# A two-layer streaming encoder step on one core: the end of the recurrence in an order of its own on each engine, and the norms between stages with ScalarE squaring from the bank, outputs weighted as they leave it, and rows taken in twos

## The chip, the core and the metric

The kernel runs on one NeuronCore of a Trainium2 chip. Five engines work at the same time, each through its own list of instructions in order: TensorE (PE, matrix products, with its weight loads PEld beside it), VectorE (DVE), ScalarE (ACT), GpSimd (POOL) and SyncE (SP, which here only issues DMAs). They meet through semaphores. The metric is the device time of one execution in microseconds; the kernel before takes 2728.57 us, the median of 3 runs.

## The reference

288 tokens (256 of a prompt, 32 of a running stream) go through two layers, D_MODEL = 2048, all in float32. Layer 0 mixes by a gated linear recurrence with 16 heads of 128, layer 1 by latent attention. Each mixer and each ConvFFN stands between two RMS norms:

```python
def rms_norm(x, w):
    y = xf * lax.rsqrt(jnp.mean(xf * xf, axis=-1, keepdims=True) + EPS)
    return (y * w.astype(F32)).astype(x.dtype)
...
    h = rms_norm(x, norm_w[layer, 0])
    m, s = hgrn2_mixer(h, ...)            # or mla_mixer in layer 1
    x = x + rms_norm(m, norm_w[layer, 1])
    f, buf = conv_ffn(rms_norm(x, norm_w[layer, 2]), ...)
    x = x + rms_norm(f, norm_w[layer, 3])
```

In the recurrence each head gives `o`, which is normalised by itself (`rms_norm(o, g_norm_w) * silu(g)`) and enters the product with `w_out` as one of its 16 rows of 128.

## The kernel before, in words

Features lie on the 128 partitions and tokens along the free axis, so an activation is 16 rows of 128x288 (`X`, `Y`). Every float32 product is made of three: a weight chunk `raw` (up to 8 blocks of 128x128, 512 KB) is split by ScalarE into `w_hi` (`split_hi`, L216) and by VectorE into the rest `w_lo` (`split_lo`, L223), and `product` runs hi*hi, hi*lo and lo*hi (L229 to L231). Chunks go round a ring of four; a chunk's `w_hi` waits until TensorE has done the chunk four before (`chunk_done`). A tile of output (128 features) is two chunks in most products; four banks of PSUM hold tiles 0 to 3 in turn.

**The recurrence** is a loop over heads. In step j TensorE makes the four input tiles of head j (`mm(0)` to `mm(7)`), while VectorE, ScalarE and GpSimd work on head r = j-1 (gates, decays, operands; `main`) and t = j-2 (scores, states, output; `tail`). Between its chunks TensorE turns values (L617), makes state updates (L625), the head's output (L634 to L639), the sum of squares of it (L646, L650), turned keys (L656) and the score products (L668 to L672). The last two steps, j = 16 and 17, are the same code with fewer parts: in j = 16 the chunks are those of the next product, `hgrn_out` (`late(0)` to `late(7)`, by `gemm_late`, rows 0 to 13 of its 16), and in j = 17 nothing is left but head 15's tail, with `late(8)` before the head's output and `late(9)`, the product of its last row, at the very end. VectorE applies the scores (`att`, L493 to L509) before TensorE may go on to the updates. SU, GS and OV, which hold updates, sum and output, lie in the same banks as the scores; TR has a bank of its own.

**Output tiles** of `hgrn_out`, `mla_out` and the four `ffn_out` phases leave the bank by ScalarE into `yt` (`out_act`, L725). VectorE copies them to `Y` (L741) or adds them (L737, second half of an FFN), squares them (L739, L742) and sums the squares (`ssq`, L744). `run_out` sets the order: the splits for tile t, then the drain of tile t-1; after the last trip three splits for the next phase, the last drain, and the fourth split.

**A norm between stages** (s = 1 to 4) begins when TensorE has summed `ssq` over partitions (L871). ScalarE loads the table set (L811), makes the reciprocal root (L806, L808), and then VectorE walks through the 16 rows: `Y` times weight and root (L880), `X` plus `Y` (L884) and, three rows behind, `h_lo` (L889). ScalarE makes `h_hi` and the square of each row (L827, L828). TensorE follows row by row (`gemm_first`): tiles 0 and 1 over rows 0 to 7, then the rest, and after chunk 6 a product with `ssx` (L290), the sum of the squares that VectorE folds at L903. Norm 1 stands behind `hgrn_out`, 2 behind the first FFN, 3 behind `mla_out`; norm 4 ends the program, and its rows go out by one DMA each (L1486).

## Time and profile before

| | |
|---|---|
| median of 3 runs | 2728.57 us (2728.56 to 2728.85) |
| the profiled execution | 2727.83 us, its span 2726.0 us |
| PE busy | 2653.6 us, 97% of the span |
| DVE, ACT, POOL busy | 1809.6, 1279.9, 410.2 us |
| HBM traffic | 406.97 MB read, 151 GB/s over the span |
| TensorE clock granted | 0.990 of full speed in the mean |

The span is from the first to the last instruction; 1.83 us lie around it. A row of the profile names the line, the engine, what is written and read, and, in brackets, how long the engine sat idle just before it and who released it. Idle time of an engine that nobody waits for costs nothing, so TensorE's idle stretches are the ones to follow here.

### The profile page before, as it was taken

The page shows a single profiled execution, that of the slowest core. Times are in us where ns is not written, and L with a number is a line of the kernel's source. Part 1 is how long each engine was busy: PE and PEld are TensorE (multiplying, and loading weights), DVE is VectorE, ACT ScalarE, POOL GpSimd, SP SyncE. Part 2 cuts the span into 40 slices and gives each one's busy share as a digit, 9 for nine tenths or more (in the row PEclk, how much of TensorE's full clock was granted, in tenths as well). Part 3 has the DMA queues.
Part 4 walks back from the last instruction along what each step waited for, and adds up shares of the span by engine and source line. Part 5 has one row for each costly group of instructions (what it writes and reads, how often), then busy time and mean ns, then how long its engine had stood idle before and what let it go on. Part 6 is the DMA issues. An engine that isn't in the chain of part 4 may idle for free.

```text
span 2726.0 us, 55560 instructions
## 1 busy us (share of the span) xinstructions
PE 2653.6 (97%) x19734; PEld 2637.2 (97%) x19734; DVE 1809.6 (66%) x3089; ACT 1279.9 (47%) x2133; POOL 410.2 (15%) x792
## 2 busy tenths in 40 slices
PE   8999999988999999999999999998999999999997
PEld 8999999988999999999999999998999999999997
DVE  7788888757766644766755855558766545666655
ACT  6555666435444433444434566535444433444432
POOL 1111112100322100222200000001322101222200
PEclk9999999999999999999999999999999999999998
DMA  6444444444555555454455422253544555445553
GB/s 230 138 140 137 143 137 130 129 136 137 165 167 165 160 165 169 160 169 162 153 175 168 147 89 81 94 169 128 179 160 165 162 166 166 165 160 168 163 164 112
DMA packets 124256, 413.58 MB, mean 152 GB/s; under 512 B 14032, under 2 KB 22384, under 8 KB 124176
## 3 DMA queue, kind: packets, MB, share of 16 engines
q1 hardware_dynamic: 116064, 406.37, 46.6%
q10 hardware_dynamic: 7056, 3.21, 0.4%
q0 software_dynamic: 1056, 2.92, 0.3%
q8 instruction: 50, 0.82, 0.1%
q14 instruction: 30, 0.25, 0.0%
HBM read 406.97 MB, written 5.48 MB: 151 GB/s over the span
## 4 chain that ended last, share of the span: by engine, by line
PE 92%; DVE 5%; ACT 1%; issue 1%; DMA 0%; POOL 0%; DVEq 0%; ACTq 0%; SPq 0%
PE bank L229 29%; PE bank L231 29%; PE bank L230 29%; DVE Y L880 1%; DVE X L884 1%; DVE w_lo L223 1%; DVE h_lo L889 1%; PE bank L669 1%; PE bank L1430 1%; PE bank L625 1%; DVE Y L903 1%; PE bank L670 0%; PE bank L634 0%; ACT w_hi L216 0%; PE bank L1435 0%
## 5 line engine op out<-in xcount | busy, mean ns | idle before, releaser
L229 PE MATMUL bank<-h_hi,w_hi 128*128 128x288 f32 (+1 forms) x4208 | 1267.4, 301 | 31.2 <-DVE h_lo L889 15.4
L230 PE MATMUL bank<-h_lo,w_hi 128*128 128x288 f32 (+1 forms) x4208 | 1251.0, 297 | 0.0
L231 PE MATMUL bank<-h_hi,w_lo 128*128 128x288 f32 (+1 forms) x4208 | 1247.2, 296 | 0.0
L216 ACT ACTIVATE w_hi<-raw 128x1024 fp32r<-128x1024 f32 (+2 forms) x786 | 807.7, 1037 | 887.1 <-PE bank L231 877.3
L223 DVE TENSOR_TENSOR w_lo<-raw,w_hi 128x1024 fp32r<-128x1024 f32 (+2 forms) x786 | 954.9, 1225 | 376.3 <-ACT w_hi L216 375.5
L229 PEld LDWEIGHTS bank<-h_hi,w_hi 128*128 128x128 f32 x4208 | 791.6, 188 | 37.8 <-issue 29.5
L231 PEld LDWEIGHTS bank<-h_hi,w_lo 128*128 128x128 f32 x4208 | 794.5, 189 | 0.2
L230 PEld LDWEIGHTS bank<-h_lo,w_hi 128*128 128x128 f32 x4208 | 792.8, 188 | 0.7
L1054 POOL TENSOR_TENSOR ext<-yt,small 128x256 f32<-128x256 f32 x176 | 213.3, 1212 | 1533.3 <-ACT yt L949 1035.8
L229 PE MATMUL bank<-g_hi,w_hi 128*128 128x288 f32 x1408 | 416.8, 296 | 0.0
L230 PE MATMUL bank<-g_lo,w_hi 128*128 128x288 f32 x1408 | 415.4, 295 | 0.0
L231 PE MATMUL bank<-g_hi,w_lo 128*128 128x288 f32 x1408 | 413.9, 294 | 0.0
L231 PEld LDWEIGHTS bank<-g_hi,w_lo 128*128 128x128 f32 x1408 | 265.1, 188 | 0.0
L230 PEld LDWEIGHTS bank<-g_lo,w_hi 128*128 128x128 f32 x1408 | 264.2, 188 | 0.0
L229 PEld LDWEIGHTS bank<-g_hi,w_hi 128*128 128x128 f32 x1408 | 263.7, 187 | 0.0
L1009 DVE TENSOR_SCALAR cv<-ext,conv_w 128x290 f32<-128x290 f32 x176 | 77.4, 440 | 216.4 <-POOL conv_new L1060 216.4
L229 PE MATMUL bank<-o_hi,w_hi 128*128 128x288 f32 x512 | 155.5, 304 | 10.8 <-DVE w_lo L223 7.7
L230 PE MATMUL bank<-o_lo,w_hi 128*128 128x288 f32 x512 | 153.7, 300 | 0.0
L231 PE MATMUL bank<-o_hi,w_lo 128*128 128x288 f32 x512 | 153.2, 299 | 0.0
L725 ACT ACTIVATE yt<-bank 128x288 f32<-128x288 f32 x105 | 43.0, 410 | 223.5 <-PE bank L231 223.5
L229 PEld LDWEIGHTS bank<-o_hi,w_hi 128*128 128x128 f32 x512 | 98.7, 193 | 12.0 <-DVE w_lo L223 8.3
L1011 DVE SCALAR_TENSOR_TENSOR cv<-ext,conv_w,cv 128x290 f32<-128x290 f32 x176 | 92.2, 524 | 24.4 <-DVE cv L1009 22.3
(247 smaller groups left out, 2141.6 us busy)
## 6 DMA issues: line engine op xcount, KB each, us to landing
raw<-in_w_fi SPq DMA_DIRECT2D x352, 512.0 KB, 4.0
raw<-in_w_hi_in SPq DMA_DIRECT2D x128, 512.0 KB, 4.2
raw<-in_w_fo SPq DMA_DIRECT2D x128, 512.0 KB, 3.5
raw<-in_w_fo SPq DMA_DIRECT2D x64, 384.0 KB, 3.2
raw<-in_w_ho SPq DMA_DIRECT2D x32, 512.0 KB, 4.1
raw<-in_w_mo SPq DMA_DIRECT2D x32, 512.0 KB, 3.9
raw<-in_w_down SPq DMA_DIRECT2D x18, 512.0 KB, 4.3
raw<-in_w_ukv SPq DMA_DIRECT2D x16, 512.0 KB, 3.8
```

Source lines behind the costliest of these rows:

```text
L216: act.activation(w_hi[:, ch.slot, 0:n], raw[:, ch.slot, 0:n], ACT.Copy).then_inc(hi_done, 1)
L223: dve.tensor_tensor(w_lo[:, ch.slot, 0:n], raw[:, ch.slot, 0:n], w_hi[:, ch.slot, 0:n].bitcast(F32), ALU.subtract).then_inc(lo_done, 1)
L229: pe.matmul(out, w_hi[:, ch.slot, w], rhs_hi, start=start, stop=False)
L230: pe.matmul(out, w_hi[:, ch.slot, w], rhs_lo, start=False, stop=False)
L231: return pe.matmul(out, w_lo[:, ch.slot, w], rhs_hi, start=False, stop=stop)
L625: su = pe.matmul(SU[:, n * P:(n + 1) * P], ktok[0:BL, n, :], vtok[0:BL, min(n, NB - 1), :], start=True, stop=True)
L669: pe.matmul(out[:, A0:A0 + 192], key_a[:, c:c + BL], z[:, OQ:BK], start=True, stop=True)
L725: act.activation(yt[:, t % 4, :], psum[t % 4][:, 0:T], ACT.Copy).then_inc(evacuated, 1)
L880: dve.scalar_tensor_tensor(out=Y[:, k, :], in0=Y[:, k, :], scalar=norm_w[:, la, wa, k:k + 1], in1=RSA, op0=ALU.mult, op1=ALU.mult).then_in ...
L1009: dve.tensor_scalar(cv[:, t, :], ext[:, t, 2:EXT], tap(2), tap(3), ALU.mult, ALU.add).then_inc(conv_step, 1)
L1011: dve.scalar_tensor_tensor(out=cv[:, t, :], in0=ext[:, t, 1:EXT - 1], scalar=tap(1), in1=cv[:, t, :], op0=ALU.mult, op1=ALU.add).then_inc( ...
L1054: pool.tensor_tensor(ext[:, t, 2:2 + TP], yt[:, t, 0:TP], RSB[:, 0:TP], ALU.mult)
```

## The change

It has three parts.

1. **The recurrence's end.** Steps 16 and 17 are replaced by one list per engine: `hgrn_end_act`, `hgrn_end_dve`, `hgrn_end_pe`. The parts of the step became functions of their own (`gate_exps` is L427 to L429 of before, `sigmoids` L431 to L433, `decay_exps` L457 to L459, `diff_exps` L465 to L469, `out_root` L472 to L474; `scores_near` and `scores_far` are L493 to L501 and L509, `differences` L550 to L564, `near_operands` and `far_operands` L576 to L581 and L591 to L593; `turn_values`, `updates`, `head_outputs`, `turn_keys`, `score_products` are the parts of `hgrn_pe`) and hold the same instructions. Head 15's updates go to TR's bank instead of SU's, and the sum of squares of head 14 is one float32 product instead of two split ones.
2. **Drains and norms.** Behind `hgrn_out` and `mla_out` ScalarE squares from the bank into `sq` and then copies from the bank to `Y` times the norm's weight; behind the second half of an FFN VectorE adds the bank to `Y`, ScalarE squares `Y` and weights it in place; the first half goes by ScalarE straight to `Y`. VectorE only sums the squares, and not the last one: TensorE adds `ones` x `ssq` and `ones` x `sq` in the bank. The table set is loaded once, behind the FFNs, ahead of the last drain. In the walk, `Y` and `X` are taken by twos (norms 1 to 3, after two single rows) or by fours and twos (norm 4).
3. **The result** goes out in five DMAs instead of 16.

The diff, cut to its core:

```diff
-            step(eng, HEADS, False, True, True)
-            step(eng, HEADS + 1, False, False, True)
+            end(eng)
+        def hgrn_end_act(act):
+            r, t = HEADS - 1, HEADS - 2
+            hi = lambda k: split_hi(act, "hgrn_out", 0, k)
+            hi(0); hi(1)
+            values_out(act, r)
+            hi(2); hi(3)
+            gates_out(act, r)
+            keys_by_token(act, t)
+            gate_exps(act, r)
+            sigmoids(act, r)
+            hi(4)
+            decay_logs(act, r)
+            hi(5)
+            decay_exps(act, r)
+            states_out(act, t)
+            diff_exps(act, r)
+            out_squares(act, t)
+            state_load(act, r)
+            values_by_token(act, r)
+            hi(6)
+            out_root(act, t)
+            keys_by_token(act, r)
+            out_top(act, t)
+            hi(7)
+            out_squares(act, r)
+            states_out(act, r)
+            out_root(act, r)
+            out_top(act, r)
+        def hgrn_end_dve(dve):
+            lo(0); lo(1); lo(2); lo(3)
+            clamp(dve, r)
+            scores_near(dve, t)
+            gates_keys_queries(dve, r)
+            scores_far(dve, t)
+            decay_sums(dve, r)
+            lo(4)
+            new_states(dve, t)
+            differences(dve, r)
+            lo(5)
+            decayed_keys(dve, r)
+            near_operands(dve, r)
+            far_operands(dve, r)
+            dve.wait_ge(S["o_raw"], t + 1)
+            decayed_queries(dve, r)
+            out_scaled(dve, t)
+            silu_gate(dve, r)
+            lo(6)
+            new_states(dve, r, TR)
+            out_rest(dve, t)
+            lo(7)
+            scores_near(dve, r)
+            scores_far(dve, r)
+            out_scaled(dve, r)
+            out_rest(dve, r)
+        def hgrn_end_pe(pe):
+            late(0)
+            turn_values(pe, r)
+            late(1)
+            late(2)
+            pe.wait_ge(S["att_ready"], t + 1)
+            updates(pe, t)
+            late(3)
+            head_outputs(pe, t)
+            late(4)
+            square_sums(pe, t)
+            turn_keys(pe, r)
+            late(5)
+            pe.wait_ge(S["k_tok"], r + 1)
+            updates(pe, r, TR)
+            score_products(pe, r)
+            late(6)
+            late(7)
+            pe.wait_ge(S["att_ready"], r + 1)
+            head_outputs(pe, r)
+            square_sums(pe, r)
+            late(8)
+            late(9)
...
         def out_act(act, phase, i, t):
+            ycol = Y[:, bass.ds(out_col(phase, i, t), 1), :]
+            bank = psum[t % 4][:, 0:T].unsqueeze(1)
+            if phase not in NORMED:
+                act.wait_ge(chunk_done, last_chunk(phase, i, t))
+                act.activation(ycol, bank, ACT.Copy).then_inc(evacuated, 1)
+                return
+            at = norm_index(phase)
+            if not (isinstance(i, int) and i == 0 and t == 0):
+                act.wait_ge(sums_done, i * TILES[phase] + ((KT - 1) * at + t))
+            if phase in FROM_BANK:
+                act.wait_ge(chunk_done, last_chunk(phase, i, t))
+                act.activation(sq[:].unsqueeze(1), bank, ACT.Square).then_inc(y_squared, 1)
+            else:
+                act.wait_ge(evacuated, tile_number(phase, i, t) + 1)
+                act.activation(sq[:].unsqueeze(1), ycol, ACT.Square).then_inc(y_squared, 1)
+            if not (isinstance(i, int) and out_col(phase, i, t) == KT - 1):
+                weighted(act, phase, i, t)
+        def out_dve(dve, phase, i, t):
+            if phase not in FROM_BANK:
+                dve.wait_ge(chunk_done, last_chunk(phase, i, t))
+                dve.tensor_tensor(ycol, ycol, psum[t % 4][:, 0:T].unsqueeze(1), ALU.add).then_inc(evacuated, 1)
+            if isinstance(i, int) and out_col(phase, i, t) == KT - 1:
+                return
+            dve.wait_ge(y_squared, i * TILES[phase] + (KT * at + t + 1))
+            dve.tensor_tensor(ssq[:], ssq[:], sq[:], ALU.add).then_inc(sums_done, 1)
...
-            load_set(act, EXP_LN_SET)
             if post:
                 rstd(act, stat[s, "post"], psum[4], RSA, D)
+                weighted(act, phase, TRIPS[phase] - 1, TILES[phase] - 1)
...
-            pe.matmul(psum[4][:, 0:T], ones[:], ssq[:], start=True, stop=True).then_inc(n_sum, 1)
+            pe.wait_ge(sums_done, (KT - 1) * s)
+            pe.matmul(psum[4][:, 0:T], ones[:], ssq[:], start=True, stop=False)
+            pe.wait_ge(y_squared, KT * s)
+            pe.matmul(psum[4][:, 0:T], ones[:], sq[:], start=False, stop=True).then_inc(n_sum, 1)
...
+            for g, (k0, n) in enumerate(groups):
+                rows = slice(k0, k0 + n)
+                dve.tensor_tensor(Y[:, rows, :], Y[:, rows, :], RSA.unsqueeze(1).to_broadcast([P, n, T]), ALU.mult)\
+                    .then_inc(y_scaled, n)
+                dve.wait_ge(y_scaled, KT * (s - 1) + k0 + n)
+                dve.tensor_tensor(X[:, rows, :], X[:, rows, :], Y[:, rows, :], ALU.add).then_inc(x_ready, n)
+                if pre and g > 0:
+                    lower(g - 1)
```

`lower(g)` is the `h_lo` step (L889 of before) for the rows of group g, with the two early splits in it as before.

On ScalarE, at the recurrence's end (Y stands for the gates here, ktok for head 14's keys by token), before:

```order
L420 ACTIVATE ktok<-bank 96x256
L421 ACTIVATE ktok<-bank 64x128
L422 ACTIVATE ktok<-bank 32x128
L216 ACTIVATE w_hi<-raw 128x1024
L427 ACTIVATE Y<-Y 128x288
L428 ACTIVATE Y<-row_tiles 128x288
L429 ACTIVATE Y<-row_tiles 128x288
L431 ACTIVATE Y<-Y 128x864
L433 ACTIVATE Y<-Y 128x864
L216 ACTIVATE w_hi<-raw 128x1024
```

and now:

```order
L414 ACTIVATE ktok<-bank 96x256
L415 ACTIVATE ktok<-bank 64x128
L416 ACTIVATE ktok<-bank 32x128
L420 ACTIVATE Y<-Y 128x288
L421 ACTIVATE Y<-row_tiles 128x288
L422 ACTIVATE Y<-row_tiles 128x288
L426 ACTIVATE Y<-Y 128x864
L428 ACTIVATE Y<-Y 128x864
L216 ACTIVATE w_hi<-raw 128x1024
L432 ACTIVATE row_tiles<-row_tiles 128x288
```

The split of the fifth chunk stood ahead of the three exponentials of the gates and the two passes of the sigmoids, and now stands behind them.

On TensorE, where the scores of head 15 are made, before:

```order
L669 MATMUL bank<-Y,row_tiles 96x192
L670 MATMUL bank<-Y 96x144
L672 MATMUL bank<-Y 96x32
L625 MATMUL bank<-vtok,ktok 128x128 x4
L229 MATMUL bank<-o_hi,w_hi 128x288
L230 MATMUL bank<-o_lo,w_hi 128x288
L231 MATMUL bank<-o_hi,w_lo 128x288
```

and now:

```order
L231 MATMUL bank<-o_hi,w_lo 128x288
L752 MATMUL bank<-vtok,ktok 128x128 x4
L792 MATMUL bank<-row_tiles 96x48
L793 MATMUL bank<-Y,row_tiles 96x192
L794 MATMUL bank<-Y 96x144
L796 MATMUL bank<-Y 96x96
L792 MATMUL bank<-row_tiles 96x48
```

Head 15's updates (ktok with vtok) stood behind its scores and now stand ahead of them; behind the scores stood the updates, and stand now the products of two chunks.

On VectorE, at the start of the walk through the rows in norm 1 (small is the reciprocal root), before:

```order
L880 SCALAR_TENSOR_TENSOR Y<-Y,norm_w,small 128x288 x2
L884 TENSOR_TENSOR X<-X,Y 128x288
L880 SCALAR_TENSOR_TENSOR Y<-Y,norm_w,small 128x288
L884 TENSOR_TENSOR X<-X,Y 128x288
L880 SCALAR_TENSOR_TENSOR Y<-Y,norm_w,small 128x288
L884 TENSOR_TENSOR X<-X,Y 128x288
L889 SCALAR_TENSOR_TENSOR h_lo<-X,norm_w,h_hi 128x288
L880 SCALAR_TENSOR_TENSOR Y<-Y,norm_w,small 128x288
```

and now:

```order
L1094 TENSOR_TENSOR Y<-Y,small 128x288
L1097 TENSOR_TENSOR X<-X,Y 128x288
L1094 TENSOR_TENSOR Y<-Y,small 128x288
L1097 TENSOR_TENSOR X<-X,Y 128x288
L1081 SCALAR_TENSOR_TENSOR h_lo<-X,norm_w,h_hi 128x288
L1094 TENSOR_TENSOR Y<-Y,small 128x576
L1097 TENSOR_TENSOR X<-X,Y 128x576
L1081 SCALAR_TENSOR_TENSOR h_lo<-X,norm_w,h_hi 128x288
L1094 TENSOR_TENSOR Y<-Y,small 128x576
```

The first `h_lo` came after seven instructions and now comes after four; the weight is no longer an operand of the first pass, and the passes over `Y` and `X` cover 576 elements from the third row on.

## Rows read from the trace of the kernel before

**Rows 1.** The page, part 1: busy time of TensorE
```profile
PE 2653.6 (97%) x19734; PEld 2637.2 (97%) x19734; DVE 1809.6 (66%) x3089; ACT 1279.9 (47%) x2133; POOL 410.2 (15%) x792
```

**Rows 2.** Waits of TensorE over the whole span: total us, times, longest
```profile
PE bank L229 <- DVE h_lo L889: 15.4, 11, 4.7
...
PE bank L229 <- DVE w_lo L223: 10.5, 6, 4.4
PE bank L871 <- DVE ssq L744: 7.4, 4, 2.0
```

**Rows 3.** Stretches: length, busy PE, PEld, DVE, ACT, POOL, clock, DMA share, GB/s
```profile
509.60:559.30 49.70, 37.82 (x267) 36.57 (x266) 32.55 (x87) 20.53 (x41) 0.92 (x1) 0.91 0.26 84
638.30:671.50 33.20, 25.92 (x171) 24.45 (x170) 31.64 (x62) 23.41 (x45) 0.00 (x0) 0.90 0.32 107
...
700.00:1400.00 700.00, 700.00 (x5252) 700.00 (x5251) 442.95 (x625) 291.10 (x409) 150.44 (x329) 1.00 0.52 165
```

**Rows 4.** Timeline of TensorE, recurrence's end: start us, duration us, what, [idle before]
```profile
519.47 1.05 PE L625 MATMUL bank<-vtok,ktok 96*128 96x128 f32 x8
...
543.20 2.03 PE L625 MATMUL bank<-vtok,ktok 96*128 96x128 f32 x8 [4.72 <-DVE lev L509]
...
553.09 0.40 PE L229 MATMUL bank<-o_hi,w_hi 128*128 128x288 f32 x1 [3.07 <-DVE o_lo L597]
...
559.32 0.61 PE L229 MATMUL bank<-o_hi,w_hi 128*128 128x288 f32 x1 [3.28 <-DVE w_lo L223]
```

**Rows 5.** Timeline of GpSimd and of ScalarE in the same stretch
```profile
509.07 1.45 POOL L681 TENSOR_TENSOR row_tiles<-row_tiles,small 128x288 f32<-128x288 f32 x1 [0.30 <-ACT row_tiles L417]
...
513.00 1.06 ACT L216 ACTIVATE w_hi<-raw 128x1024 fp32r<-128x1024 f32 x1 [3.32 <-PE bank L231]
...
549.18 0.45 ACTq L447 DMA_DIRECT2D o_hs<-s_new  x1
```

**Rows 6.** Timeline of VectorE in the same stretch
```profile
540.68 2.37 DVE L509 COPY_PREDICATED lev<-level_mask,bank 96x144 f32<-96x144 uint32 x6 [0.47 <-issue]
...
558.05 2.35 DVE L223 TENSOR_TENSOR w_lo<-raw,w_hi 128x1024 fp32r<-128x1024 f32 x2
```

**Rows 7.** Timeline around norm 1: ScalarE, VectorE, TensorE
```profile
638.67 1.05 ACT L216 ACTIVATE w_hi<-raw 128x1024 fp32r<-128x1024 f32 x1
...
642.04 0.95 DVE L880 SCALAR_TENSOR_TENSOR Y<-Y,norm_w,small 128x288 f32<-128x288 f32 x2 [0.91 <-ACT small L808]
...
644.87 0.51 DVE L889 SCALAR_TENSOR_TENSOR h_lo<-X,norm_w,h_hi 128x288 fp32r<-128x288 f32 x1
645.30 0.51 DVE L880 SCALAR_TENSOR_TENSOR Y<-Y,norm_w,small 128x288 f32<-128x288 f32 x1
645.73 0.45 DVE L884 TENSOR_TENSOR X<-X,Y 128x288 f32<-128x288 f32 x1
646.10 0.51 DVE L889 SCALAR_TENSOR_TENSOR h_lo<-X,norm_w,h_hi 128x288 fp32r<-128x288 f32 x1
...
666.23 4.74 DVE L903 TENSOR_TENSOR Y<-Y 128x2304 f32<-128x2304 f32 x3
...
671.52 0.51 PE L290 MATMUL bank<-ssx,ones 128*128 128x288 f32 x1 [0.35 <-DVE ssx L903]
```

**Rows 8.** Durations of VectorE additions by size in norm 1
```profile
L903 DVE TENSOR_TENSOR Y<-Y x3: 757/1359/2551, 666.2 to 670.2; 128x2304 f32<-128x2304 f32 x1, 128x1152 f32<-128x1152 f32 x1, 128x576 f32<-128x576 f32 x1
```

**Rows 9.** Timeline: ScalarE before norm 2, TensorE in mla_out
```profile
1495.70 0.41 ACT L725 ACTIVATE yt<-bank 128x288 f32<-128x288 f32 x1 [1.28 <-PE bank L231]
...
1497.07 1.28 ACT L811 ACT_TABLE_LOAD   x1
...
1770.48 0.61 PE L229 MATMUL bank<-o_hi,w_hi 128*128 128x288 f32 x1 [4.42 <-DVE w_lo L223]
```

**Rows 10.** Timeline of norm 4 on VectorE, and its DMAs
```profile
2710.88 0.95 DVE L880 SCALAR_TENSOR_TENSOR Y<-Y,norm_w,small 128x288 f32<-128x288 f32 x2 [1.85 <-ACT small L808]
...
o_y<-X SPq DMA_DIRECT2D x16, 144.0 KB, 1.7
```

More of the change, by code:

```diff
@@ new lines, in turn_values, with updates @@
+        def turn_values(pe, r):
+            pe.wait_ge(S["scaled"], 4 * r + 3)
+            if past_first(r):
+                pe.wait_ge(S["k_tok"], r)
+            for n in range(NB):
+                tr = pe.transpose(TR[0:BL, n * P:(n + 1) * P], vfm[:, n * BL:(n + 1) * BL], ident[:])
+            tr.then_inc(S["v_turned"], 1)
+        def updates(pe, t, su=SU):
+            for n in range(NB + 1):
+                up = pe.matmul(su[:, n * P:(n + 1) * P], ktok[0:BL, n, :], vtok[0:BL, min(n, NB - 1), :], start=True, stop=True)
+            up.then_inc(S["updates"], 1)
@@ L709, in trunk_program @@
-        for name, trips, _, tiles in order:
-            if "out" in name or "down" in name:
-                mode = {"hgrn_out": "only", "mla_out": "only", "down": "first"}.get(name)
-                mode = mode or ("first" if name.endswith("0") else "add")
-                y_count[name] = (n_done, n_kept, n_sq, mode)
-                n_done += trips * tiles
-                n_kept += trips * tiles if mode == "add" else 0
-                n_sq += trips * tiles if mode != "first" else 0
         TRIPS = {name: trips for name, trips, _, _ in order}
+        NORMED = {"hgrn_out": (0, 1), "ffn_out01": (0, 3), "mla_out": (1, 1), "ffn_out11": (1, 3)}
@@ L719, in out_act, with norm_index @@
+        FROM_BANK = ("hgrn_out", "mla_out")
+        def norm_index(phase):
+            return list(NORMED).index(phase)
         def out_act(act, phase, i, t):
[L720 to L725 removed]
@@ L748, in run_out @@
+        def run_out(eng, phase, split, drain, ahead=lambda: None):
             trips, n = TRIPS[phase], TILES[phase]
@@ L762, in run_out @@
             split_next(eng, split, phase, (0, 1, 2))
+            ahead()
             drain(eng, phase, trips - 1, n - 1)
@@ L932, in ffn_act @@
             stats = half == 0 and isinstance(i, int) and i == 0
-            before = {(0, 0): "hgrn_out", (0, 1): "ffn_out00", (1, 0): "mla_out", (1, 1): "ffn_out10"}[layer, half]
-            y_before = y_count[before][0] + TRIPS[before] * TILES[before]
             def hi(t):
```

607 lines of the change are left out of this document (323 added, 284 removed).

## The prediction

> **What bounds the kernel now.** I read the page first: TensorE is busy for 2653.6 us of the 2726.0 us span [rows 1], so all there is to gain lies in the 72 us in which it is idle and in the time at the lower clock. The table of its waits comes next: 15.4 us for `h_lo`, 10.5 us for `w_lo`, 7.4 us for `ssq` [rows 2]. The table by stretch tells where: in an FFN the engine never stops (5252 products in 700 us, so they start 0.133 us apart, at 2.4 GHz), while the recurrence's end has 37.8 us of work in 49.7 us, at a granted clock of 0.91 [rows 3]. The timelines of single stretches give the rest. I work from five places: the recurrence's end, norms 1 to 3 with the drains ahead of them, the start of `mla_out`, norm 4, and everything else as cover.
>
> **1. The recurrence's end.** Before, TensorE starts `late(0)` at 509.6 and the first product of the next trip at 559.32. Its idle pieces in between are 4.72 us (scores of head 15), about 0.8 us in two small waits, 3.07 us (last row) and 3.28 us (first `w_lo` of the next trip) [rows 4], 11.9 us in sum, as rows 3 have it (49.70 less 37.82). Three pieces run at 1.2 GHz: the updates at 543.20 take 2.03 us where those of head 14 took 1.05 us [rows 4], and two times 12 products 0.11 us longer each; some 3.5 us less the few that were fast already, so 3.0. That leaves 49.7 - 11.9 - 3.0 = 34.8 us of work.
> The new order, by the durations of before: the exponentials of the gates waited until 514.0 behind a split that had itself waited 3.32 us for TensorE, until 513.00 [rows 5]; their own input is there at 509.07 + 1.45 = 510.5 [rows 5]. So gates, sigmoids, decays and differences all come 3 to 5 us earlier; on TensorE the scores need no wait and come 3.6 us earlier, at 531.9, for the updates (0.9 us) now stand ahead of them and the two chunks of `late(6)` and `late(7)` (2 x 18 products, 4.8 us) behind. VectorE needs 4.5 us from the scores' end to the last mask (from 543.20 - 4.72 = 538.5 to 540.68 + 2.37 = 543.05 [rows 4, 6]), and these 4.8 us hide it: the wait of 4.72 us goes, and the slow clock behind it. What is late next is the chain behind head 15's output. From 549.2, where its sum of squares starts and ScalarE issues the second DMA, to the last row at 553.09 are 3.9 us [rows 4, 5]: sum, root, two VectorE steps, `o_hi` and `o_lo`. TensorE's own 0.6 us in it and `late(8)`, 1.6 us, which now follows the sum, hide 2.2; the root waits 0.2 for the two DMA issues, as the sum now runs fast: 1.9 us idle is left. Then the drains of the first trip. ScalarE squares tile 0, VectorE sums it, and only then may the next square start: 0.41 + 0.46 and two hand-overs, 0.95 us per tile, but VectorE has one addition per tile and not three instructions. I take the square and the weighting at the 0.41 us of the copy from the bank [rows 9]; 0.5 each would add 0.3. First `w_lo`: 0.6 + 2 x 0.95 + 0.85 (square and weighting of the third tile) + 1.05 + 1.2 = 5.5 us behind the start of `late(9)`, against 559.32 - 553.09 = 6.2 us; idle 3.9 us, and slow behind it as before. New time: 34.8 + 0.35 (float32 sum instead of split) + 0.5 (square) + 0.15 (turned keys wait for `vtok`) + 1.9 + 3.9 = 41.6 us, against 49.7: **-8.1 us**. In the chain three hand-overs have a slack of only 0.1 to 0.5 us (keys by token, last mask, `w_lo` of the eighth chunk). Ends: each late by a microsecond, -5; all of the wait at `late(9)` hidden, -10.
>
> **2. Drains and norms 1 to 3.** Behind `hgrn_out` the chain was: ScalarE copy, three VectorE steps, L871, table load, root, first row at 642.04 [rows 7]. Squares now come from ScalarE alone, the sum over 15 tiles is in the bank before the last one comes, and the load is gone. But the fourth split of the next phase stands between: `w_hi` at 638.7 for 1.05 us [rows 7], `w_lo` behind it for 1.2 (2.35 for two [rows 6]), until 641.0, and VectorE starts its rows there: -1.0 us (norm 3 alike). In norm 2 VectorE's addition stays ahead of the square, so the split starts 0.5 us later: -0.7.
> The walk. From first row to L290 it took 671.52 - 642.04 = 29.5 us [rows 7]: per row 0.43 (L880) + 0.37 (L884) + 0.43 (L889) = 1.23 [rows 7], 16 of them, four splits 4.5 us, the fold 5.2 us. Now a pair has `Y`, on which `X` waits at once: 0.757 us for 576 elements [rows 8] and 0.03, then 0.67, then two `h_lo`, 0.86: 2.31 us, 1.16 per row. 7 pairs, two single rows of 1.29 each, splits and fold: 28.6 us, **-0.9 each**. The first `h_lo` is ready at 2.2 us instead of 3.3 us, row 7 at 11.1 instead of 11.9. TensorE has 120 products (16.0 us) between row 7 and L290 and could be there at 28.0, so VectorE's fold still decides, and a slow clock in rows 0 to 7 is hidden up to 0.6 us. Sum: norms 1 and 3 -1.9 each, norm 2 -1.6: **-5.4 us**. Ends: nothing from the walk, -2.7; the fold no longer last, -7.
> On size the Trainium skill (VectorE: DVE Perf Modes, "The TRN2 errata") says that a fixed latency is paid per instruction and is worth amortising over 512 elements and more; its fixed term of 151 cycles fits the rows within 2 ns (757 and 1359 ns [rows 8]). Paid in full for each of the 14 instructions saved per norm, that would be an estimate of 2.2 us a norm. The rows show 0.43 and 0.37 from start to start where the durations are 0.51 and 0.45 [rows 7], so most of it was overlapped before, and I stay with 0.9.
> The table load of 1.28 us [rows 9] behind the FFNs now stands before the last drain, where ScalarE sat idle for 1.28 us before its copy [rows 9] and now waits 0.5 us longer for VectorE: hidden. The Trainium skill (ScalarE: Activation LUTs, "What ACT_TABLE_LOAD costs") counts 2.66 us for a switch, with a drain; by that, 0.9 us would show in norm 2 and my sum would be 0.9 less.
>
> **3. Start of `mla_out`.** TensorE waits 4.42 us for `w_lo` [rows 9], from 1766.06, behind three drains on VectorE. By the count of part 1 (first bank full 1.1 us before that, 2 x 0.95 + 0.85 + 1.05 + 1.2 = 5.0) it comes at 1769.9 instead of 1770.48: **-0.6**. Ends 0 and -1.
>
> **4. Norm 4.** No split stands in it: TensorE's wait of 2.0 us for `ssq` [rows 2] becomes an addition (0.46) and a square (0.41): the first row comes 1.0 us earlier than 2710.88 [rows 10]. No rows after it feed TensorE. 16 rows took 16 x 0.80 = 12.8 us (0.43 + 0.37 [rows 7]). Fours take 1.36 + 0.02 + 1.27 = 2.65, twos 1.45: 3 x 2.65 + 2 x 1.45 = 10.9 us, -1.9. The last DMA is twice as large; at the 1.7 us to landing for 144 KB [rows 10] I add 0.5. **-2.4**. Ends -1.2 and -3.
>
> **Everything else.** ScalarE gets two instructions per tile (0.9 us) and loses one, VectorE loses two or three. Both are far from full in the FFN (443 and 291 us of 700 [rows 3]), and a chunk's `w_lo` is ready some 3 us after the drain, while TensorE has 6.4 us of work or more ahead: nothing, but about 0.3 us per tile if that cover were gone.
>
> **Sum**: 8.1 + 5.4 + 0.6 + 2.4 = 16.5 us. 2727.83 - 16.5 = 2711.3 for an execution like the profiled one; the median of the runs is 0.7 us above it, so **2712 us**, 0.6% faster.
>
> **Rivals.**
> A. *The clock.* With rows in twos TensorE gets 12 products in 2.3 us, with gaps, and may stay at 1.2 GHz until row 7: 48 products cost 0.24 each, row 7 ends at 14.6 instead of 12 and L290 comes at 30.6 instead of 28.6. Against it: over norm 1 the clock was 0.90 [rows 3], so 6.6 of 33.2 us stood at the low level, most of them before the first row; it rose while the rows came singly, with gaps. Three norms lose 2.0 each: 2718. The Trainium skill (TensorE: Matmul & The Clock Gate, Part 1) calls the low rate the default that activity releases; it speaks for this rival, and no row shows rows in twos.
> B. *A new wait in the recurrence's end.* ScalarE's list is strict: `decay_exps` waits for head 14's states, so the differences' exponentials may come late, the scores with them, and the 4.8 us of cover are spent. Half of part 1 goes: 2716.
> C. *More than that.* After shorter idle stretches the clock stays up where trips start (2.1 us each at `hgrn_out` and `mla_out`), and half of the last-row wait is hidden: 2707.
> D. *Slower.* TensorE stays at 1.2 GHz through norms 1 to 3 beyond row 7. That costs rival A's 2.0 us and 120 x 0.107 = 12.8 us a norm, in full 44 us: 2756. It decides from 33 slow products behind row 7 in each norm, where 16.5 us are spent. 48 products without a gap follow row 7, which speaks against it.
> E. *The walk gains nothing*, since the wait of `X` on `Y` shows in full on each pair: -2.7 us less gain, 2715.
>
> **Chances.** Forecast 0.50 (2709 to 2714 its own range), A 0.14, B 0.12, C 0.10, E 0.11, D 0.03. From 2706 to 2719 leaves out D and the tails of the others, together below 0.2, and takes in the ends of each part taken singly. A difference under about 0.2% (5.5 us) can't be told from none here: faster by more needs below 2723. All single cases but D stand there; A, B and E together would reach it, 0.03: faster 0.94, same 0.03, slower 0.03.
>
> **What would show it.** Right: no wait of TensorE for the masks (4.72 us before) and the first product of the next trip near 551; the exponentials of the gates at 510.6; L290 28.6 us behind the first row of each norm; the first row of norm 1 right behind the fourth `w_lo`; 10.9 us for norm 4's rows. Wrong: a new TensorE wait above 1 us between 527 and 540; L290 with TensorE never waiting for it (rival A); VectorE pairs longer than 2.4 us; a table load between the last drain and a root.

## The result, and the profile after

The changed kernel takes 2712.19 us (median of 5 runs, 2711.43 to 2713.47) against 2728.57 us (5 runs, 2728.05 to 2730.66): a ratio of 0.9937, 95% interval 0.9926 to 0.9948, 16.4 us less. The forecast was 2712. The profiled execution has a span of 2711.6 us, 14.4 less than before. Below, "after" is this kernel.

The page's first part and TensorE's waits over the span, as in [rows 1, 2]:

```profile
PE 2656.3 (98%) x19742; PEld 2639.2 (97%) x19742; DVE 1759.4 (65%) x2892; ACT 1300.3 (48%) x2173; POOL 410.7 (15%) x792
```
```profile
PE bank L229 <- DVE h_lo L1081: 12.1, 8, 3.7
...
PE bank L229 <- DVE w_lo L223: 10.5, 6, 3.8
...
PE bank L1068 <- ACT sq L905: 1.2, 2, 0.6
PE bank L290 <- DVE ssx L1111: 0.9, 3, 0.3
```

`h_lo` went from 15.4 to 12.1 us, the wait of 7.4 us for `ssq` became 1.2 us for `sq`, and the masks (4.72 us, [rows 4]) have no row any more. `w_lo` is where it was in sum.

To place the gain I cut both traces at the same instructions: start of `late(0)`, first product behind the wait at the next trip, last product of `hgrn_out` (or of the FFN, or of `mla_out`), first row of the norm on VectorE, and L290.

| from, to (us) | before | after | difference | forecast |
|---|---|---|---|---|
| start, `late(0)` | 509.47 | 510.88 | +1.41 | 0 |
| `late(0)`, next trip's first product | 49.85 | 40.92 | -8.93 | -8.1 |
| to the last product of `hgrn_out` | 78.71 | 78.29 | -0.42 | 0 |
| last product, first row: norms 1 and 3, each | 4.01 | 2.93 | -1.08 | -1.0 |
| the same, norm 2 | 4.06 | 3.44 | -0.62 | -0.7 |
| first row, L290: norms 1 to 3, each | 29.48 | 29.15 | -0.33 | -0.9 |
| L290 of norm 2, first product of the next trip in `mla_out` | 241.54 | 240.90 | -0.64 | -0.6 |
| to the last product of `mla_out` | 78.97 | 79.07 | +0.10 | 0 |
| last product, first row of norm 4 | 4.08 | 3.24 | -0.84 | -1.0 |
| first row of norm 4, end | 15.12 | 13.81 | -1.31 | -1.4 |

The two FFNs take 823.86 us each, as before (823.85). The rows sum to -14.4 us, which is the span's. The first is no work of the change. Both kernels begin with the same list of products, 0.24 us apart at 1.2 GHz; before, the clock rises at 14.06 us (the duration falls from 0.44 to 0.35), after it does so at 17.06, some 12 products later, each 0.107 us longer, and the first had started 0.12 us later. TensorE's timeline of before, then of after:

```profile
13.82 0.44 PE L230 MATMUL bank<-h_lo,w_hi 128*128 128x288 f32 x1
14.06 0.35 PE L231 MATMUL bank<-h_hi,w_lo 128*128 128x288 f32 x1
```
```profile
16.82 0.43 PE L230 MATMUL bank<-h_lo,w_hi 128*128 128x288 f32 x1
17.06 0.33 PE L231 MATMUL bank<-h_hi,w_lo 128*128 128x288 f32 x1
```

In the eleven kernels below the clock rose between 14.2 and 17.1 us, with the same instructions up to there. Without that row the change gave 15.8 us in the traces.

The stretches that answer to [rows 3] (length, busy PE, PEld, DVE, ACT, POOL, clock, DMA share, GB/s): the recurrence's end, the rest of `hgrn_out`, norm 1.

```profile
510.88:551.80 40.92, 35.09 (x269) 34.23 (x267) 30.50 (x80) 20.34 (x42) 1.03 (x1) 1.00 0.31 102
551.80:630.09 78.29, 78.29 (x576) 78.29 (x577) 35.96 (x38) 32.94 (x48) 0.00 (x0) 0.98 0.51 168
630.09:662.17 32.08, 27.55 (x175) 25.50 (x174) 29.40 (x45) 21.50 (x38) 0.00 (x0) 0.89 0.36 115
```

TensorE is idle for 5.8 us of the recurrence's end, where it was 11.9, and the clock is 1.00 where it was 0.91. Its three waits there, on TensorE's timeline (answering to [rows 4]), and the exponentials of the gates on ScalarE's ([rows 5]):

```profile
542.27 0.75 PE L769 MATMUL bank<-yt,ones 128*128 128x288 f32 x2 [0.50 <-ACT yt L436]
...
546.10 0.40 PE L229 MATMUL bank<-o_hi,w_hi 128*128 128x288 f32 x1 [1.49 <-DVE o_lo L671]
...
551.80 0.40 PE L229 MATMUL bank<-o_hi,w_hi 128*128 128x288 f32 x1 [3.84 <-DVE w_lo L223]
```
```profile
511.95 0.44 ACT L420 ACTIVATE Y<-Y 128x288 f32<-128x288 f32 x1 [0.86 <-POOL row_tiles L860]
```

ScalarE's drains of the first trip (L902 square, L915 weighted copy), which replace L725, and what stands behind them:

```profile
546.80 0.41 ACT L902 ACTIVATE sq<-bank 128x288 f32<-128x288 f32 x1 [1.25 <-PE bank L231]
547.11 0.50 ACT L915 ACTIVATE Y<-bank,norm_w 128x288 f32<-128x288 f32 x1
547.81 0.41 ACT L902 ACTIVATE sq<-bank 128x288 f32<-128x288 f32 x1 [0.20 <-DVE ssq L930]
...
548.74 0.41 ACT L902 ACTIVATE sq<-bank 128x288 f32<-128x288 f32 x1
...
549.43 2.00 ACT L216 ACTIVATE w_hi<-raw 128x1024 fp32r<-128x1024 f32 x2
```

Squares follow each other after 1.01 and 0.94 us; `w_hi` waits behind three of them, and TensorE for its `w_lo`.

Norm 1 on VectorE (answering to [rows 7]): two single rows, a pair in the middle, the fold; then L290 on TensorE.

```profile
633.02 0.45 DVE L1094 TENSOR_TENSOR Y<-Y,small 128x288 f32<-128x288 f32 x1
...
633.50 0.46 DVE L1097 TENSOR_TENSOR X<-X,Y 128x288 f32<-128x288 f32 x1
...
637.13 0.75 DVE L1094 TENSOR_TENSOR Y<-Y,small 128x576 f32<-128x576 f32 x1
637.99 0.76 DVE L1097 TENSOR_TENSOR X<-X,Y 128x576 f32<-128x576 f32 x1
638.66 0.94 DVE L1081 SCALAR_TENSOR_TENSOR h_lo<-X,norm_w,h_hi 128x288 fp32r<-128x288 f32 x2
639.52 0.75 DVE L1094 TENSOR_TENSOR Y<-Y,small 128x576 f32<-128x576 f32 x1
...
656.88 4.74 DVE L1111 TENSOR_TENSOR Y<-Y 128x2304 f32<-128x2304 f32 x3
```
```profile
662.17 0.75 PE L290 MATMUL bank<-ssx,ones 128*128 128x288 f32 x2 [0.30 <-DVE ssx L1111]
```

Start to start `Y` takes 0.86 us, `X` 0.67, two `h_lo` 0.86: 2.39 us a pair.

### The profile page after: what moved, and what is told of

Its sections match the earlier page's. It is cut to its first block, busy times and chain, and to the rows that moved or that the text cites. A ratio compares the mean times of both kernels' runs of the same rounds, so it can differ in the third digit from the quotient of the medians.

```text
span 2711.6 us, 55304 instructions
## 1 busy us (share of the span) xinstructions
PE 2656.3 (98%) x19742; PEld 2639.2 (97%) x19742; DVE 1759.4 (65%) x2892; ACT 1300.3 (48%) x2173; POOL 410.7 (15%) x792
## 4 chain that ended last, share of the span: by engine, by line
PE 93%; DVE 5%; ACT 1%; issue 1%; DMA 0%; POOL 0%; SPq 0%; DVEq 0%; ACTq 0%
PE bank L229 30%; PE bank L231 29%; PE bank L230 29%; DVE w_lo L223 1%; DVE X L1097 1%; DVE Y L1094 1%; DVE h_lo L1081 1%; PE bank L793 1%; PE bank L1638 1%; PE bank L752 1%; DVE Y L1111 1%; ACT w_hi L216 0%; PE bank L794 0%; PE bank L759 0%; PE bank L1643 0%
## 5 line engine op out<-in xcount | busy, mean ns | idle before, releaser
L229 PE MATMUL bank<-h_hi,w_hi 128*128 128x288 f32 (+1 forms) x4208 | 1270.2, 302 | 28.2 <-DVE h_lo L1081 12.1
L229 PEld LDWEIGHTS bank<-h_hi,w_hi 128*128 128x128 f32 x4208 | 794.2, 189 | 35.1 <-issue 26.7
L1214 DVE SCALAR_TENSOR_TENSOR cv<-ext,conv_w,cv 128x290 f32<-128x290 f32 x176 | 92.2, 524 | 24.4 <-DVE cv L1212 22.3
L1217 DVE SCALAR_TENSOR_TENSOR cv<-ext,conv_w,cv 128x290 f32<-128x290 f32 x176 | 91.8, 522 | 22.5 <-DVE cv L1214 6.2
```

The lines of the kernel that those rows point to most:

```text
L229: pe.matmul(out, w_hi[:, ch.slot, w], rhs_hi, start=start, stop=False)
L1214: dve.scalar_tensor_tensor(out=cv[:, t, :], in0=ext[:, t, 1:EXT - 1], scalar=tap(1), in1=cv[:, t, :], op0=ALU.mult, op1=ALU.add).then_inc( ...
L1217: dve.scalar_tensor_tensor(out=cv[:, t, :], in0=ext[:, t, 0:EXT - 2], scalar=tap(0), in1=cv[:, t, :], op0=ALU.mult, op1=ALU.add).then_inc( ...
```

## The experiments

All are timed against the kernel before, which took 2728.57 us at the median beside after, 2728.72 beside e1 to e4, 2729.55 beside e5 to e8 and 2730.12 beside e9 to e11. A difference between a run and after crosses these sets, so it holds to 1 to 1.5 us. Differences of stretches are read from the profiled executions at the marks of the table above.

**e1: the recurrence's end alone.** On the kernel before:

```diff
-            step(eng, HEADS, False, True, True)
-            step(eng, HEADS + 1, False, False, True)
+            end(eng)        # hgrn_end_act, hgrn_end_dve, hgrn_end_pe
```

> The kernel before with nothing but the recurrence's end in its new order; drains, norms and outputs as before. Theory (the parts add up): the end gives its 8.9 us of the after trace less what its new drains give (squares on ScalarE instead of three instructions on VectorE). From late(0) to the first product of the next trip 41.5 us (49.7 before, 40.8 after); everything behind as before, L290 33.5 us behind the last product. About 8 us below before: ratio 0.9970. Rival (the clock stays up at the trip's start only because of the shorter drains): then the first products of the next trip are at 0.44 us again and the stretch from there to the last product is 78.7 us, not 78.3. Rival (most of the gain at the trip's start belongs to the drains): 43 us or more for the stretch.

2719.72 us, ratio 0.9965 (0.9951 to 0.9978), 9.0 us less than before. The stretch took 41.32 us and the rest of `hgrn_out` 78.28; norms and `mla_out` as before. So the end alone makes 8.5 us and also the 0.4 us of clock behind it. Both rivals fall: the clock gain is there without the new drains, and these add only 0.4 us here (41.32 to 40.92).

**e2: everything but that.** On after:

```diff
-            end(eng)
+            # the parts of steps 16 and 17 in the order of before, on each engine
```

> The kernel after with the recurrence's end in its old order on all engines; the new drains, norms and outputs stay. Theory: what is left of the change is norms 1 to 3 (1.4 + 1.0 + 1.4 us in the after trace), the start of mla_out (0.6), norm 4 (2.1) and about 0.8 at the first trip's start: 6.5 to 7.5 us below before, ratio 0.9975, and TensorE's wait of 4.7 us for the masks of the last head is back. Rival (the prediction's own sizes, 0.9 us per norm for the walk): 8 to 8.5 us below before, and the after trace lost that to its late clock at the start.

2721.22 us, ratio 0.9971 (0.9960 to 0.9983), 7.5 us less than before at the median. The wait for the masks is back at 4.71 us. In the trace 6.8 us are gained from `late(0)` on, with norms 1 to 3 exactly as in after. The two halves give 9.0 and 7.5 us and the whole 16.4: they add up. The stretches bear out the theory; the median stands at its upper end.

**e3: rows one at a time.** On after:

```diff
-            if stages[s][1]:
-                return [(0, 1), (1, 1)] + [(k, 2) for k in range(2, KT, 2)]
-            return [(k, 4) for k in range(0, KT - 4, 4)] + [(KT - 4, 2), (KT - 2, 2)]
+            return [(k, 1) for k in range(KT)]
```

> The kernel after with its rows one at a time in all four norms, in the order Y, X, h_lo of the row before; 16 output transfers. Theory (a dependent X waits 0.48 us behind its Y, by the single rows of the after trace at 633.02 and 633.50): 0.48 + 0.38 + 0.43 = 1.29 us per row, so from the first row to L290 some 1.2 us longer than in pairs (30.3 against 29.15), slower per row than the 1.23 of before, which kept its rows three apart; norm 4 takes 16 x 0.86 = 13.8 us for its rows against 11.35. In all 3 x 1.2 + 2.4 - 0.4 = 5.6 us above after, ratio to before about 0.996. Rival (pairs gain by their count, 0.9 us per norm against the old walk): 29.5 us, as before. Clock: with single rows TensorE's first products come 1.29 us apart per six; theory that pairs keep it at 1.2 GHz longer (6.4 us in the after trace, 3.5 before): here about 3.5 us again.

2723.75 us, ratio 0.9982 (0.9973 to 0.9991): 11.6 us above after, twice what I expected. VectorE in norm 1:

```profile
641.40 0.46 DVE L1095 TENSOR_TENSOR X<-X,Y 128x288 f32<-128x288 f32 x1
641.77 0.52 DVE L1079 SCALAR_TENSOR_TENSOR h_lo<-X,norm_w,h_hi 128x288 fp32r<-128x288 f32 x1
642.20 0.45 DVE L1092 TENSOR_TENSOR Y<-Y,small 128x288 f32<-128x288 f32 x1
642.69 0.46 DVE L1095 TENSOR_TENSOR X<-X,Y 128x288 f32<-128x288 f32 x1
```

The price of a row is as said, 0.49 + 0.37 + 0.43 = 1.29 us, and norm 4's span part is 16.01 us. But L290 comes 32.1 to 32.3 us behind the first row, 3 more than in after and not 1.2. Of the stretch up to the fold, 26.8 us, rows and splits make 16 x 1.29 + 4.5 = 25.1; most of the rest, 1.3 us, are waits of `w_lo` and `h_lo` for ScalarE around the early splits. What they are came out in e5. The clock rose 5.5 to 6.2 us behind the first product, as in after (6.2 to 6.6) and not as before (2.9 to 3.8): the pairs are not the reason.

**e4: the scores behind `late(6)` and `late(7)`.** On after:

```diff
-            score_products(pe, r)
             late(6)
             late(7)
+            score_products(pe, r)
```

> The kernel after with one edit: TensorE issues the scores of the last head behind late(6) and late(7) and not ahead of them. Theory (these 4.8 us of products are what hides the masks): TensorE waits 4.4 to 4.8 us for the last mask (L574), and the products behind the wait run at 1.2 GHz; the stretch from late(0) to the next trip takes 40.8 + 4.6 + 1 = 46 to 47 us, the whole 5 to 6 us more than after, ratio to before about 0.996. Rival (the earlier gates alone make the end short, and the masks' chain has slack): under 2 us more.

2718.63 us, ratio 0.9962 (0.9949 to 0.9975), 6.4 us more than after. The stretch took 48.42 us, 7.5 more, and the rest of `hgrn_out` 79.34, 1.1 more. TensorE's row of the wait:

```profile
544.45 1.17 PE L759 MATMUL bank<-lev,vtok 96*128 96x96 f32 x4 [4.23 <-DVE lev L574]
```

and what follows the wait, up to the next trip, in e4 and then in after:

```profile
544.45:558.24 13.79, 9.58 (x38) 8.58 (x38) 4.38 (x9) 6.46 (x14) 0.00 (x0) 0.62 0.03 10
```
```profile
540.35:551.80 11.45, 5.62 (x40) 4.94 (x38) 4.38 (x9) 6.45 (x14) 0.00 (x0) 1.00 0.04 11
```

The masks' wait is back with 4.23 us, and the slow clock with it: at a granted clock of 0.62 and not 1.00 TensorE is busy 4.0 us longer there, of which 1.6 come back as shorter waits, so the stretch is 2.3 us longer; and 1.1 us more are lost in the next trip. With 0.4 for the `w_lo` of `late(6)`, which now comes earlier, that is all but 0.6 us of the 8.6 in the trace (which is the longest of the five executions; the median has 6.4). The cover is what took the wait away. It is worth twice the wait in this trace, and one and a half times by the medians.

**e8: the gates behind the split again.** On after:

```diff
+            hi(4)
             gate_exps(act, r)
             sigmoids(act, r)
-            hi(4)
```

> The kernel after with one edit on ScalarE: the split of chunk 4 of hgrn_out stands ahead of the exponentials and sigmoids of the gates again, as before the change. Theory (the earlier gates carry part 1, since everything of head 15 hangs on them): the exponentials start at 514 to 515.4 instead of 511.95, the scores come 2.5 to 3.5 us later, TensorE waits for them (the cover of late(6) and late(7) lies behind the scores and can't help), and the stretch from late(0) to the next trip takes 43.5 to 44.5 us, 3 us more than after. Rival (the chain has slack once the scores stand ahead of late(6)): under 1 us more, and the whole of part 1 is TensorE's own order.

2715.75 us, ratio 0.9949 (0.9934 to 0.9964). The exponentials start 4.5 us behind `late(0)` (514.20), where they stand 1.1 behind it in after, and the stretch takes 44.45 us, 3.5 more. The number is that of the theory, the place is not: TensorE never waits for what head 15's scores read. It waits for the masks of head 14, which VectorE's list has behind `clamp`, and `clamp` waits for the exponentials. VectorE's `clamp`, then TensorE's updates of head 14:

```profile
515.33 0.61 DVE L582 TENSOR_SCALAR Y<-Y 128x864 f32<-128x864 f32 x1 [3.44 <-ACT Y L422]
```
```profile
521.62 1.16 PE L752 MATMUL bank<-vtok,ktok 96*128 96x128 f32 x8 [1.75 <-DVE lev L574]
```

The wait is 1.75 us, and behind it the clock was 0.50 from 523.3 to 526.6, which costs 1.7 more: that is all of the 3.5. In the order of after, part 1 so needs both edits, the earlier gates (3.5 us) and the cover for the masks (7.5 us). Whether late gates would still cost anything with `clamp` behind head 14's masks, where it stood before, was not tested.

**e5: `h_lo` of the pair before between `Y` and `X`.** On after:

```diff
+            for g in range(last + 1):
+                weigh(g)                 # Y of group g
+                if g > 1:
+                    lower(g - 1)         # its h_lo, with the early split behind rows 10 and 13
+                add(g)                   # X of group g
+                if g == 1:
+                    lower(0)
+            lower(last)                  # norm 4: Y of g+1, X of g
```

> The kernel after with VectorE's rows in another order: between Y of a pair and the X that waits for it stand the two h_lo of the pair before (norms 1 to 3), or Y of the next group (norm 4). Theory (the walk in pairs lost its gain to X waiting 0.86 us behind Y where 0.67 would do, 0.19 per pair): pairs 2.20 us apart instead of 2.40, first row to L290 28.0 us instead of 29.15 (then TensorE's own products, 25 of them at 1.2 GHz, decide as well), 1.1 us for each of norms 1 to 3, and 0.4 for norm 4: 3.7 us below after, 2708.5. Rival (TensorE's slow clock in the first rows decides L290 already): L290 moves by no more than the 0.30 us that TensorE waits for ssx, 1.3 us in all. Rival (h_lo now waits for h_hi of the row before, which ScalarE has ready only 1.1 us behind X): pairs stay 2.4 us apart, no gain.

2722.02 us, ratio 0.9973 (0.9962 to 0.9984): 10 us more than after, where 3.7 less was expected. Pairs do come 2.22 us apart, and norm 4 gained 0.7 us (13.12 for 13.81). But L290 comes 32.3 us behind the first row. VectorE and ScalarE at row 10 of norm 1:

```profile
645.26 0.52 DVE L1081 SCALAR_TENSOR_TENSOR h_lo<-X,norm_w,h_hi 128x288 fp32r<-128x288 f32 x1
647.20 1.23 DVE L223 TENSOR_TENSOR w_lo<-raw,w_hi 128x1024 fp32r<-128x1024 f32 x1 [1.43 <-ACT w_hi L216]
648.34 0.51 DVE L1081 SCALAR_TENSOR_TENSOR h_lo<-X,norm_w,h_hi 128x288 fp32r<-128x288 f32 x1
648.77 0.75 DVE L1103 TENSOR_TENSOR X<-X,Y 128x576 f32<-128x576 f32 x1
```
```profile
646.13 1.04 ACT L216 ACTIVATE w_hi<-raw 128x1024 fp32r<-128x1024 f32 x1
649.56 0.54 ACT L1023 ACTIVATE h_hi<-X,norm_w 128x288 fp32r<-128x288 f32 x1 [2.39 <-DVE X L1103]
```

VectorE waits for `w_hi`, which ScalarE makes behind the square of that pair; the next `X` stands behind the waiting `w_lo`, and ScalarE's next `h_hi` waits for that `X`. Each engine waits for the other in turn: VectorE's waits for ScalarE in norm 1 are 1.43, 1.00, 0.60 and 1.00 us. TensorE then waits 3.12 us for `h_lo` near the end.

**e6: two splits of the next trip ahead of the drains,** in `hgrn_out` and `mla_out`. On after:

```diff
+                    if early and isinstance(i, int) and i == 0 and t in (1, 2):
+                        split(eng, phase, 1, t - 1)      # trip 1 then leaves these two out
                     if t > 0 or before:
                         drain(eng, phase, i if t else i - 1, t - 1 if t else n - 1)
```

> The kernel after with the first two splits of the next trip of hgrn_out and mla_out ahead of the first two drains of the trip before, not behind the third. Theory (TensorE waits 3.84 and 3.83 us at these two places for w_lo alone, and that stands behind three drains of 0.94 us each only by its place in the lists): w_hi starts at 546.8 in the time of the after trace instead of 549.43, TensorE restarts 2.6 us earlier at both places, 5.2 us in all: 2707. Rival (the drained bank or the second chunk is late instead): 1 to 2 us of the 5.2 come back as waits of TensorE within the next 7 us.

2703.78 us, ratio 0.9904 (0.9889 to 0.9919), 8.4 us below after. TensorE's waits fall from 3.84 to 1.34 us, 2.5 at each place, 0.1 less than expected. The rest is clock: both trips run without a slow product, 1.5 and 2.3 us shorter than in after (78.29 and 79.07), and no new wait of TensorE follows in them. That makes 8.8 us in the traces, of which 0.2 are lost again ahead of norm 2; the medians have 8.4. The two stretches behind the waits:

```profile
548.29:625.05 76.76, 76.76 (x575) 76.76 (x576) 37.43 (x41) 35.29 (x54) 0.00 (x0) 1.00 0.52 171
1752.20:1828.97 76.77, 76.77 (x576) 76.77 (x576) 37.42 (x41) 35.29 (x54) 0.00 (x0) 1.00 0.52 171
```

**e7: both edits.**

> Both of the two edits (rows' order on VectorE, splits ahead of drains) on the kernel after. Theory: they lie in different stretches and add up: 3.7 + 5.2 = 8.9 us below after, 2703.3, ratio to before 0.9907. Rival: the sum of what each shows alone, whatever that is, less a part where the longer work of TensorE meets later splits.

2714.02 us, ratio 0.9942 (0.9928 to 0.9955): 1.8 above after, where e5 and e6 alone give +9.8 and -8.4. Within the spread of the sets they add up as the rival has it; the loss of e5 stays.

**e9 and e10: taking the ring apart.** e9 is e7 with the early `w_lo` one `Y` later; e10 keeps the rows further apart, as the kernel before did:

```diff
+            weigh(0)
+            for g in range(last + 1):
+                if g < last:
+                    weigh(g + 1)
+                add(g)
+                if g > 0:
+                    lower(g - 1)
+                    early(g - 1)         # e9: weigh(g), early(g - 2), lower(g - 1), add(g)
+            lower(last)
```

> The kernel of e7 (h_lo of the pair before between Y and X; two splits ahead of the drains) with one edit: VectorE takes the two early w_lo of the next phase (behind rows 10 and 13) one Y later, after the next X has been issued and not before it. Theory (e5 and e7 lost 3.2 us a norm because w_lo waited 1.43 us there for ScalarE's w_hi, X behind it, and ScalarE's h_hi behind X, a ring that e3 shows as well): without that ring pairs stay 2.22 us apart to the end, L290 comes 28.0 us behind the first row (29.15 in after, 32.3 in e5), 1.1 us for each of three norms and 0.7 for norm 4 (13.12 us in e5 against 13.81): 4 us below e6, ratio to before 0.989. Rival (TensorE's clock, 1.2 GHz for 4 to 6.6 us in the first rows, decides instead of VectorE): 29.0 us, and TensorE doesn't wait for ssx. Rival (ScalarE is full there: h_hi 0.96, square 0.67 and two splits): the wait moves to h_lo or to the next w_lo, over 29.5 us.

> As e9, but with the rows kept apart as in the kernel before: Y of the next group, X of this one, h_lo of the one before, then its early split. Theory: the same 2.2 us per pair and no ring, as every wait is for something a whole instruction older; the first h_lo comes 0.4 to 0.5 us later than in after. L290 28.0 to 28.3 us behind the first row. If e9 still shows waits and this one doesn't, the ring is a matter of the distance between Y, X and h_lo, not of ScalarE's load. Rival as for e9: TensorE decides, 29 us.

e9 took 2701.96 us, ratio 0.9897 (0.9880 to 0.9913), e10 2701.29 us, ratio 0.9895 (0.9879 to 0.9912). L290 comes 28.6 and 28.3 us behind the first row, where after has 29.15 and e5 32.3: the order of two splits was worth 3.7 us a norm. VectorE in e10, norm 1, and L290 there:

```profile
637.61 0.75 DVE L1106 TENSOR_TENSOR Y<-Y,small 128x576 f32<-128x576 f32 x1
638.28 0.75 DVE L1113 TENSOR_TENSOR X<-X,Y 128x576 f32<-128x576 f32 x1
638.95 0.95 DVE L1088 SCALAR_TENSOR_TENSOR h_lo<-X,norm_w,h_hi 128x288 fp32r<-128x288 f32 x2
639.81 0.76 DVE L1106 TENSOR_TENSOR Y<-Y,small 128x576 f32<-128x576 f32 x1
```
```profile
657.21 0.65 PE L290 MATMUL bank<-ssx,ones 128*128 128x288 f32 x2
```

Pairs are 2.20 us apart, and TensorE comes to L290 without a wait, though `ssx` is there at 655.92 + 0.46 = 656.38: now TensorE is the bound, but not by its clock, as the rival had it. The clock rose 6.0, 3.7 and 5.5 us behind the first product of norms 1 to 3, and L290 stands at 28.3 us in each: TensorE has caught up with the rows by row 6, 10.65 us behind the first row, and from there its 132 products run without a gap, 17.6 us. In e9 VectorE still is (a wait of 1.01 us for `ssx`, and `w_lo` waits 0.56 once). e10 is the fastest kernel here, 10.9 us below after at the medians.

**e11: the table load where it was.** On after:

```diff
             post, pre = stages[s]
+            load_set(act, EXP_LN_SET)    # and no longer ahead of the last drain
```

> The kernel after with the table load back where it was, between the last drain and the root, in all four norms. Theory (a load takes 1.28 us on ScalarE, the row of the trace, and nothing else): norms 1 and 3 +0.9 each (1.28 less the 0.37 us in which the root waited for VectorE's w_lo anyway), norms 2 and 4 +0.45 each (the load starts when the square ends, 0.85 us ahead of the end of its sum): 2.7 us above after. By the Trainium skill (ScalarE: Activation LUTs, What ACT_TABLE_LOAD costs), which counts 2.66 us for a switch with its drain, it would be an estimate of +2.3 and +1.8, 8.2 us in all. Rival (a load of the set that is already in place costs nothing in norms 1 and 3, where no other function came between): +0.9 in all.

2716.43 us, ratio 0.9951 (0.9935 to 0.9968), 4.2 us above after. The first row came 1.14, 1.15, 1.14 and 0.47 us later in norms 1 to 4, 3.9 in all. (The trace as a whole is only 2.9 us longer, for the clock happened to rise earlier in `mla_out`, worth 1.0.) So the rival falls, the load is not free in norms 1 and 3. ScalarE's timeline of norm 1:

```profile
630.72 1.05 ACT L216 ACTIVATE w_hi<-raw 128x1024 fp32r<-128x1024 f32 x1
631.79 1.28 ACT L999 ACT_TABLE_LOAD   x1
633.08 0.50 ACT L994 ACTIVATE small<-bank,eps 128x288 f32<-128x288 f32 x1
```

A load costs its 1.28 us and no more: the root starts 0.01 us behind it, in norm 2 too, where ScalarE really changes sets. The 2.66 us that the Trainium skill counts for a switch (ScalarE: Activation LUTs, "What ACT_TABLE_LOAD costs") are not seen. I had left out that in norm 2 a split stands between square and load, so the load starts too late to hide there.

## Why the prediction was right, point by point

**The recurrence's end: right in mechanism, 0.8 us low.** Forecast 41.6 us in 34.8 of work, 1.9 and 3.9 idle and small terms; the trace has 35.1 busy, 0.50 + 1.49 + 3.84 = 5.83 idle, 40.9 in all. The wait for the masks went because products stand in front of it (e4), the gates' exponentials came as early as their input (511.95 less the late start of 1.4 is 510.55, forecast 510.6). What e8 adds is that their being early pays at head 14's masks; the way to head 15's scores, which the prediction had in mind, had 2.2 us of room in after (the last of their inputs that hang on the gates was ready at 530.62, the scores began at 532.81). The wait for the last row was sized at 1.9 and is 1.49. From `late(9)` to the next trip it took 5.70 us, forecast 5.5. What I had wrong is the clock: "slow behind it as before". The nine products from 551.80 on, and all in front, ran at 2.4 GHz; it fell at 553.18 and was back at 556.3, 13 slow products where before had 18: 0.42 us less in the trip. e1 shows this to belong to the new end. It is the piece of rival C (more than that) that came true; in `mla_out` the wait still is 3.83 us and the clock behind it as slow as ever.

**Drains and first rows: right.** -1.08, -0.62, -1.08 against -1.0, -0.7, -1.0, and the first row at 633.02 is right behind the fourth `w_lo` (631.86 for 1.23 us). `mla_out` -0.64 against -0.6.

**The walk: the step that failed.** I had 2.31 us for a pair, with "`Y`, on which `X` waits at once: 0.757 us and 0.03". It is 0.86: the next instruction starts 0.67 us behind one of 576 elements if it waits for nothing of it, and 0.86 if it reads its result. The prediction's own sign of being wrong was a pair above 2.4 us, and 2.39 stands just below it. Seven pairs at 0.08 are the 0.56 us that the walk came out longer, -0.33 instead of -0.9 in each norm, 1.7 us in all. This is rival E (the walk gains little since `X` waits for `Y`), in mechanism right and in size two thirds. e10 gives the proof: with another instruction between, pairs take 2.20 us and the norm 28.3. My rivals did not have the larger danger, the ring over the early splits (e3, e5), which after escapes by little: in norm 1 its early `w_lo` starts at 648.66, and the `w_hi` it needs was done at 648.45.

**Rival A (the clock) is half true and costs nothing.** TensorE stays at 1.2 GHz for 6.4, 6.6 and 6.2 us behind its first product, where it was 3.5, 2.9 and 3.8. But L290 stands at 29.15 us in every kernel with this walk, whether the clock rose after 3.4 us (norm 2 of e4) or after 8.5 (norm 1 of e8): VectorE's fold decides, and TensorE waits 0.30 us for it or, in the latter, nothing. "Hidden up to 0.6 us" was the right reading.

**Norm 4: right.** -0.84 and -1.31 against -1.0 and -1.4. The rows took 11.35 us and not 10.9, again since `X` waits for its `Y`, but what follows the last row grew by 0.2 us where I had added 0.5. The group of the larger output DMAs (count, size, median us from issue to landing), answering to [rows 10]; the two of 288 KB took 2.1 us:

```profile
o_y<-X SPq DMA_DIRECT2D x3, 576.0 KB, 2.8
```

**Rivals B and D** did not come. No wait above 0.5 us arose between the start of the stretch and `late(9)`.

**The sum.** The terms gave 16.5 us, the stretches 15.8 and the medians 16.4. That the forecast met the median is partly luck: the end was 0.8 us better and its clock 0.4, the walks were 1.7 us worse and norm 4 0.25.

## What to carry to other kernels

When two instructions of one engine depend on each other, count the dependent distance from a row that shows it, not the duration plus a hand-over; and place an independent instruction between them, if it waits for no third engine. Where two engines take turns (rows on one, splits on both), follow one element through both lists before moving anything: a split that waits holds up all that stands behind it, and through that the engine that would release it. A wait of TensorE is worth more than its length, since the slow clock comes with it: 4.2 us of wait came with 3.4 us more of slow work in e4 (in the longest of its five executions; 2.2 by the median), and 2.5 us taken off each of two waits gave 8.4 in e6. How much the clock adds differs between executions: in e11 it gave back 1.0.
